# Value pages of five decode sequences: from the merge stage into the prompt's attention

## The reference

```python
k_past = pool_kv[l, page_table, :, 0].reshape(DB, past, FOX_H, HD)
v_past = pool_kv[l, page_table, :, 1].reshape(DB, past, FOX_H, HD)
r_past = swapaxes(cumsum(lf_past, axis=1, reverse=True) - lf_past, 1, 2)
s_p = einsum('bqhd,bshd->bhqs', q, k_past) * scale + a_new[..., None] + r_past[..., None, :]
s_n = einsum('bqhd,bshd->bhqs', q, kv[:, :, 0]) * scale + ...      # the new token's own key
p = masked_softmax(concatenate([s_p, s_n], -1))
o = einsum('bhqs,bshd->bqhd', p[..., :past], v_past) + einsum(..., p[..., past:], kv[:, :, 1])
```

## Time and profile before

| | us |
|---|---|
| median of 3 runs | 1461.28 |
| lowest and highest | 1459.33, 1465.89 |
| the profiled execution, whole | 1460.96 |
| its span | 1459.2 |
| PE busy in the span | 1209.6 (83%) |
| DVE busy | 801.3 (55%) |
| ACT busy | 240.1 (16%) |
| POOL busy | 173.7 (12%) |

### The profile page before, as it was taken

The page is one execution under the profiler, slowest core; times in us unless marked ns, Lnnn a source line. Parts: engine busy times, 40 slices in busy tenths (PEclk is TensorE's granted clock), DMA queues, the critical chain, the costliest instruction groups (busy, mean ns, idle before and its releaser), DMA issues. The chain is left out here.

```text
span 1459.2 us, 27607 instructions
## 1 busy us (share of the span) xinstructions
PE 1209.6 (83%) x10095; PEld 824.0 (56%) x10095; DVE 801.3 (55%) x1186; ACT 240.1 (16%) x681; POOL 173.7 (12%) x149
## 2 busy tenths in 40 slices
PE   0755677999999687998878998989796979798995
PEld 0755566886887474555556875546463645454241
DVE  1344340398999833456672457485857586725023
ACT  0000041112111201334451110100101010100113
POOL 0000000110000000000004031405050505040000
PEclk9968878999999765889999999989998999998898
DMA  8898504277888715100008449798978788676740
GB/s 224 243 305 245 198 31 145 88 240 231 282 268 300 198 23 203 44 1 1 1 1 262 136 143 324 232 304 259 318 233 278 239 296 275 229 235 212 265 190 30
DMA packets 205702, 282.01 MB, mean 193 GB/s; under 512 B 21614, under 2 KB 126599, under 8 KB 205119
## 3 DMA queue, kind: packets, MB, share of 16 engines
q1 hardware_dynamic: 109758, 202.40, 41.4%
q10 hardware_dynamic: 89376, 60.01, 14.3%
q0 software_dynamic: 6432, 17.83, 3.8%
HBM read 273.26 MB, written 11.11 MB: 195 GB/s over the span
## 5 line engine op out<-in xcount | busy, mean ns | idle before, releaser
L1581 PE MATMUL bank<-xnT,e_wg 128*128 128x260 f32 x1152 | 280.8, 402 | 0.5 <-DMA e_wg<-in_w_in 0.5
L1581 PEld LDWEIGHTS bank<-xnT,e_wg 128*128 128x128 f32 x1152 | 227.3, 200 | 76.5 <-issue 28.5
L585 PE MATMUL score_banks<-xnT,oT 128*128 128x260 f32 (+1 forms) x864 | 198.2, 388 | 9.9 <-DMA oT<-in_w_in 9.9
L1565 POOL DMA_INDIRECT d_slc<-in_cache_nsa_slc,selrow x128 | 154.5, 1207 | 380.2 <-PE score_banks L1652 336.1
L585 PEld LDWEIGHTS score_banks<-xnT,oT 128*128 128x128 f32 (+1 forms) x864 | 162.3, 190 | 40.3 <-DMA oT<-in_w_in 10.1
L249 PE MATMUL score_banks<-c_cols,c_w 64*64 64x64 f32 (+1 forms) x4096 | 96.5, 253 | 96.0 <-issue 57.0
L249 PEld LDWEIGHTS score_banks<-c_cols,c_w 64*64 64x64 f32 x4096 | 91.6, 166 | 100.7 <-issue 100.7
L1589 PE MATMUL bank<-oT,e_wb 128*128 128x512 f32 x192 | 101.1, 676 | 23.3 <-DVE cst L1843 11.8
L299 DVE COPY c_cols<-oT 128x1024 f32<-128x1024 f32 x48 | 48.9, 1146 | 101.2 <-DMA oT<-in_cache_nsa_cmp 82.0
L1614 PE MATMUL bank<-d_vpage,d_pf 128*8 128x512 f32 x512 | 80.0, 637 | 20.5 <-DMA d_vpage<-in_cache_fox_kv 20.5
L1589 PEld LDWEIGHTS bank<-oT,e_wb 128*128 128x128 f32 x192 | 40.0, 216 | 82.8 <-issue 82.6
(11 more groups left out here) (367 smaller groups left out, 1430.5 us busy)
## 6 DMA issues: line engine op xcount, KB each, us to landing
d_vpage<-in_cache_fox_kv SPq DMA_DIRECT2D x256, 256.0 KB, 4.7
d_kpage<-in_cache_fox_kv SPq DMA_DIRECT2D x96, 256.0 KB, 5.2
oT<-in_cache_fox_kv SPq DMA_DIRECT2D x80, 256.0 KB, 4.0
mt<-in_cache_fox_kv SPq DMA_DIRECT2D x80, 256.0 KB, 3.7
e_wg<-in_w_in ACTq DMA_DIRECT2D x36, 512.0 KB, 6.0
oT<-in_cache_nsa_cmp SPq DMA_DIRECT2D x128, 128.0 KB, 3.8
oT<-in_w_in ACTq DMA_DIRECT2D x13, 1024.0 KB, 7.9
oT<-in_cache_nsa_cmp ACTq DMA_DIRECT2D x64, 128.0 KB, 3.6
```

Of the source, the lines that this page charges most:

```text
L585: last = nc.tensor.matmul(pj[ch.n % 2][i][0:ch.w, 0:NM if ch.mem else TH], w[:, c, ch.off:ch.off + ch.w], rhs, start=c == 0, stop=c == DC - 1)
L1565: nc.gpsimd.indirect_dma_start(out=slc[:, n, :], out_offset=None, in_=k.cache_slc, in_offset=bass.IndirectOffsetOnAxis(ap=k.selrow[:, at:a ...
L1581: last = nc.tensor.matmul(gate_bank[n % 2][:, 0:TH], wg[product % WR][:, c, :], k.xnT[:, c, part * TH:(part + 1) * TH], start=c == 0, stop ...
```

## The change

The five early-scored sequences leave the last stage's fox work.

- In `middle`, their 5 x 32 pages of scores become probabilities at once: DVE adds the cumulated gates to `k.sfe`, takes the maximum per sequence and head, PE transposes and spreads it, DVE subtracts, ACT takes Exp, DVE sums, PE adds over partitions, DVE multiplies by the reciprocal. The last hidden product is cut in three pieces, with the new PE steps between them, and some copies and additions on DVE move up.
- In `prompt`, SP loads their 160 value pages into `mt` (four groups of two pages), and PE multiplies one quad of pages ahead of the transposes of each of the units 4 to 48, with a fold (adding the bands and turning) after each sequence's eight quads. The output transfers are issued between the page loads, one after every third quad. `mt` is no longer a buffer for transposed probabilities: two tiles `f_pt0`, `f_pt1` with three instead of four tiles of rows take its place, and the fourth tile of a unit is copied apart into a free corner of the tile. There is one output bank instead of two; the other holds the page sums.
- In `sample_and_merge`, key scores of the three late sequences run in steps 0 to 5, their fox softmax in steps 2, 4 and 6, their values in steps 3 and 4, 5 and 6, and 7. The other steps' softmax covers three kinds. The tail has no page values. `w_out` is loaded in two halves, the first when the last key page has been scored.

```diff
@@ middle, PE @@
-                hidden(3)
+                hidden(3, 0, 8)
+                te.wait_ge(x_max, 1)
+                te.wait_ge(grow_done, 2)
+                nc.tensor.transpose(fox_max, fmx[:, :, :].rearrange("p b h -> p (b h)"), k.ident).then_inc(x_turned, 1)
+                hidden(3, 8, 12)
+                te.wait_ge(x_dia, 1)
+                nc.tensor.matmul(fox_spread, k.ones[0:EH, :], fdia[:, :], start=True, stop=True).then_inc(x_spread, 1)
+                hidden(3, 12)
...
+                te.wait_ge(x_rden, 1)
@@ middle, ACT @@
+                sc.wait_ge(x_shifted, 1)
+                nc.scalar.activation(k.sfe[:, :, :, :], k.sfe[:, :, :, :], ACT.Exp).then_inc(x_exp, 1)
@@ middle, DVE @@
+                nc.vector.tensor_tensor(early, early, k.rpast[:, 0:EARLY * PAGES, :].rearrange("p (b n) h -> p b n h", b=EARLY), ALU.add).then_inc(x_scored, 1)
...
+                nc.vector.tensor_reduce(fmx[:, :, :], by_head, AX, ALU.max).then_inc(x_part, 1)
...
+                nc.vector.tensor_tensor(early, early, over_pages(fox_spread), ALU.subtract).then_inc(x_shifted, 1)
...
+                ve.wait_ge(x_exp, 2)
+                nc.vector.tensor_reduce(fden[:, :, :], by_head, AX, ALU.add).then_inc(x_part, 1)
...
+                nc.vector.tensor_tensor(early, early, frd[:, :, :].unsqueeze(2).to_broadcast([P, EARLY, PAGES, H]), ALU.mult).then_inc(x_done, 1)
@@ prompt, SP @@
-                for dst, src in outs:
+                left = list(outs)
+                for at in range(0, EARLY * PAGES, 2 * KV):
...
+                        if i % KV == 0 and n >= VG:
+                            sp.wait_ge(v_free, n - VG + 1)
+                        sp.dma_start(vpage[:, (n % VG) * KV + i % KV, :].unsqueeze(1),
+                                     k.cache_fox[bass.ds(pg, 1), :, 1, :].rearrange("a p n -> p a n")).then_inc(v_in[n % VG], 16)
+                    if at // (2 * KV) % 3 == 2 and left:
+                        sp.dma_start(*left.pop(0)).then_inc(out_done, 16)
@@ prompt, PE @@
-                    bank, done = o_bank[u.group % 2], ends_group(u)
-                    if u.group >= 2 and u.kind != "win":
-                        te.wait_ge(o_out[u.group % 2], u.group // 2)
+                    bank, done = o_bank, ends_group(u)
+                    if u.group and u.kind != "win":
+                        te.wait_ge(o_out[(u.group - 1) % 2], (u.group - 1) // 2 + 1)
...
+                    for i in range(4):
+                        n, page = (b * PAGES + 4 * g + i) // KV, 4 * g + i
+                        if i % KV == 0:
+                            te.wait_ge(v_in[n % VG], 16 * KV * (n // VG + 1))
+                        last = nc.tensor.matmul(fv_bank[32 * i:32 * i + H, :], k.sfe[:, b, page, :], vpage[:, (n % VG) * KV + i % KV, :],
+                                                start=g == 0, stop=g == QUAD - 1, skip_group_check=True)
...
+                    if u.no in work_of:
+                        b, g = work_of[u.no]
+                        if g < QUAD:
+                            page_values(b, g)
+                        else:
+                            fold(b)
                     turn(u)
@@ sample_and_merge @@
-        first_step = lambda b: 1 + (b - EARLY) * GROUPS // PER
+        first_step = lambda b: (b - EARLY) * GROUPS // PER
+        fox_of = {first_step(b) + 2: b for b in range(EARLY, NB)}
...
+            if b + 2 < NB:
+                values_at[b + 1] = (fox_no(b), 0, GROUPS // 2)
+                values_at[b + 2] = (fox_no(b), GROUPS // 2, GROUPS)
+            else:
+                values_at[b + 1] = (fox_no(b), 0, GROUPS)
...
                 small_values(LASTB)
+                turn_fox(sums_after[LASTB], LASTB - 1)
                 turn_sums(LASTB - 1)
-                page_values(LASTB, 0, 3)
                 y_products(0, 0)
-                page_values(LASTB, 3, 5)
                 y_products(0, 1)
-                page_values(LASTB, 5, 8)
                 y_products(1, 0)
```

More of the change, by code:

```diff
@@ L876, in _, with hidden @@
             def _(te):
-                def hidden(i):
+                def hidden(i, begin=0, end=STEP):
                     te.wait_ge(w1_in[i % 3], 64 * (i // 3 + 1))
                     te.wait_ge(tokens_done, 2)
-                    for d in range(STEP):
+                    for d in range(begin, end):
                         for v in range(2):
@@ L961, in _ @@
                                  start=True, stop=True).then_inc(v_done, 1)
+                te.wait_ge(x_den, 1)
+                nc.tensor.matmul(fox_den, k.ones, fden[:, :, :].rearrange("p b h -> p (b h)"), start=True, stop=True).then_inc(x_spread_den, 1)
                 te.wait_ge(kp_out, 2)
@@ L1205, in prompt, with turned_parts, probability @@
         both = lambda u: k.score_banks[:, 2 * (u.no % 2):2 * (u.no % 2) + 2, 0:u.n]
-        pt_bank, o_bank = ps[4:6], ps[6:8]
-        def transposed(u, j):
-            if u.kind == "mem":
-                return pt[u.set_no % 2][:, 0, 0:u.n // P, u.tile(j) * P:(u.tile(j) + 1) * P]
-            return pt[u.set_no % 2][:, j, 0:u.n // P, u.t * P:(u.t + 1) * P]
+        pt_bank, o_bank, fv_bank = ps[4:6], ps[6], ps[7]
+        of_turned = fv_bank[:, 0:8]
+        def turned_parts(u, j):
+            at = u.tile(j) * P
+            own = pt[u.set_no % 2][:, 0 if u.kind == "mem" else j]
+            tiles = min(u.n // P, 3)
+            parts = [(own[:, 0:tiles, at:at + P], in_bank(u, j)[:, 0:tiles])]
+            if u.n // P == 4:
+                parts.append((own[:, 1, 0:P], in_bank(u, j)[:, 3]))
+            return parts
+        def probability(u, j, t):
+            own = pt[u.set_no % 2][:, j]
+            return own[:, 1, 0:P] if t == 3 else own[:, t, t * P:T]
         def result(u):
@@ L1223, in _ @@
             def _(sp):
-                for dst, src in outs:
+                left = list(outs)
+                for at in range(0, EARLY * PAGES, 2 * KV):
+                    _, pages = nc.values_load_multi_w_load_instructions(k.table[0:1, at:at + 2 * KV], engines=[sp.engine], min_val=0, max_val=POOL - 1)
+                    for i, pg in enumerate(pages):
+                        n = (at + i) // KV
+                        if i % KV == 0 and n >= VG:
[4 more added lines that the diff above has]
+                        sp.dma_start(*left.pop(0)).then_inc(out_done, 16)
+                for dst, src in left:
                     sp.dma_start(dst, src).then_inc(out_done, 16)
@@ L1308, in place @@
                         ve.wait_ge(o_done, u.set_no - 1)
-                    nc.vector.tensor_copy(transposed(u, 0), in_bank(u, 0)).then_inc(pt_left, 1)
+                    for dst, src in turned_parts(u, 0):
+                        last = nc.vector.tensor_copy(dst, src)
+                    last.then_inc(pt_left, 1)
                 def result_out(u):
@@ L1342, in place @@
                         sc.wait_ge(o_done, u.set_no - 1)
-                    nc.scalar.activation(transposed(u, 1), in_bank(u, 1), ACT.Copy).then_inc(pt_right, 1)
+                    for dst, src in turned_parts(u, 1):
+                        last = nc.scalar.activation(dst, src, ACT.Copy)
+                    last.then_inc(pt_right, 1)
                 def result_out(u):
@@ L1656, in turn_sums @@
                 def turn_sums(b):
-                    te.wait_ge(of_out, b + 1)
                     te.wait_ge(os_out, b * 2 + 2)
-                    after(te, placed, b * 4)
-                    for c in range(4):
-                        nc.tensor.matmul(of_turned[:, 2 * c:2 * c + 2], fvs[:, c * P:(c + 1) * P], k.fold[:, 2 * c:2 * c + 2], start=True, stop=True)
+                    after(te, placed, b * 2)
                     for br in range(2):
@@ L1665, in turn_sums, with turn_fox @@
                     last.then_inc(sums_turned, 1)
+                def turn_fox(f, b):
+                    te.wait_ge(of_out, f + 1)
+                    te.wait_ge(placed, b * 2)
+                    after(te, fox_placed, f * 2)
+                    for c in range(4):
+                        last = nc.tensor.matmul(of_turned[:, 2 * c:2 * c + 2], fvs[:, c * P:(c + 1) * P], k.fold[:, 2 * c:2 * c + 2], start=True, stop=True)
+                    last.then_inc(fox_turned, 1)
                 def y_products(t, i, chunks=range(DC)):
-                    te.wait_ge(wout_in, 16)
+                    te.wait_ge(wout_in, 32)
                     te.wait_ge(mt_done, 2 * DC)
```

277 lines of the change are left out of this document (187 added, 90 removed).

## The result

The changed kernel takes 1477.1 us (median of 4 runs, 1473.68 to 1489.01), the kernel before 1462.24 beside it: a ratio of 1.0126 with a 95% interval of 1.0089 to 1.0162 (the medians alone give 1.0102). Slower by a little over 1%, where +10 us on 1461, 0.7%, was forecast. The profiled execution of the changed kernel took 1473.68, its span is 1471.9, 12.7 above that of the kernel before.

The account below looks back on a forecast made before the run. PE was taken to bound the prompt stage and the first part of last-stage steps, DVE their second part. Middle +4.5, prompt +49.5 and last stage -44 gave +10 on 1460.96: 1471 us, range 1442 to 1500.

Parts of the forecast that it names:

- Middle stage: Middle stage: added DVE passes mostly lie in waits, Exp and the sum behind it do not; +4.5 us, bounds 1 to 8.
- The term for the Exp: Middle stage: Exp on ScalarE, estimated at 1.4 to 2.9 us, has no cover and delays the block scores.
- Quads, folds, filled waits: Prompt stage: quads, first quads and folds add 53.1 us of PE work; filling PE's waits for ScalarE's copy returns 16.6.
- Clock: Prompt stage: filled pauses bring back some half-clock time, -7 us, bounds -13 to +13.
- The rival by the clock: Prompt stage: quads with few columns raise half-clock time from about 54 to over 100 us; 1491 or 1498; chance 0.13.
- Queue: Prompt stage: page loads wait behind outputs on SP's queue, +18 us, bounds 0 to 25; half-clock restart afterwards +2.
- Pages "just enough": Prompt stage: refilling a freed page buffer takes 7.9 us, within the 8.3 of two units, without slack.
- Last stage: Last stage: steps -25 us with the clock, tail -19; sum -44, bounds -58 to -30.
- Step 6: Last stage: without 18.3 us of key scores PE bounds all of this step, so it gains 8 us, not 18.
- Step 0: Last stage: takes 18.3 us of key scores on DVE, free because DVE waits 31.3 us there for the gates.
- The tail: End of last stage: the last sequence's page values leave the output products, -19 us, bounds -14 to -23.
- Step 7: Last stage: selected rows are asked for earlier, shortening DVE's 12.8 us wait; -5 us, between 0 and -10.

Follow-up runs that it names:

- run 4: Kernel before, value pages of the first five sequences neither loaded nor multiplied in the last stage: 1447.7 us, ratio 0.9897.
- run 5: Kernel before, the last sequence's value pages in the tail neither loaded nor multiplied: 1440.3 us, ratio 0.9898.
- run 8: Changed kernel with a ring of twelve pages, and the window state's copy and the fox rows issued in the middle stage: 1450.8 us, ratio 0.9955.
- run 6: Changed kernel with the window state's copy issued at the end of SP's list in the middle stage: 1467.0 us, ratio 1.0060.
- run 1: Changed kernel with the window state's copy issued by ScalarE on its own queue at unit 34: 1484.6 us, ratio 1.0126.
- run 11: Changed kernel with the window state's copy issued by GpSimd as one transfer of long pieces: 1485.0 us, ratio 1.0176.
- run 10: Changed kernel with the window state's copy issued by GpSimd as two transfers in pieces of 512 B: 1470.6 us, ratio 1.0081.
- run 2: Changed kernel with PE waiting for all four pages of a quad before its first product: 1483.4 us, ratio 1.0139.
- run 7: Changed kernel with a ring of twelve value pages in the prompt stage in place of eight: 1472.6 us, ratio 1.0120.
- run 12: As run 8, with SP issuing a value group ahead of the key groups in each last-stage step: 1451.2 us, ratio 0.9931.
- Run 3: Changed kernel with only the first eight value pages loaded in the prompt stage, all products kept, outputs issued at its start: 1440.6 us, ratio 0.9863.

## Why the prediction was right, and where it was off

The forecast was 1471 and its range held the time. The balance that decided it is shown: quads removed from the last stage's steps give back about a third of their PE time (run 4), the tail all of it (run 5), and in the prompt stage they are on the path (run 8: +30.9 us with no wait left). That the sum came within 3 us is luck, though: the terms below missed on both sides.

- **Middle stage**, +2.0 against +4.5. The term for the Exp was too large: it took 1.27 us, and DVE waited 0.7 there. The reductions took 2.45 us, not 1.43; a pass of the key scores was the wrong row for a reduction across the pages. The waits of the earlier trace rows covered the difference: of their 20.0 us only the last is left, with 4.6, and one of 3.7 has come.
- **Quads, folds, filled waits**: 53.1 less 16.6, nearly as worked out: with no wait for pages (run 8) PE is idle for 6.5 us of the stage, 21.2 before, so 14.7 of the 16.6 were filled. No wait of the transposes for ScalarE's copy was left.
- **Clock**, -7. By the granted clock of the stage (0.87 to 0.92) half-clock time fell from 55 to 44 us, of which some 12 are the long wait itself; that is some 10 us won. The rival by the clock did not come.
- **Queue**, +18 and +2: 15.1 in one wait, 19.4 in all, where and as long as worked out, just behind the state copy; the next longest, 2.7, follows the 2 MB of fox rows (issued at 648.77), where 3 was worked out. After the long wait PE ran at half clock for 5 us, which costs some 2.5 by half (an estimate). The reason was only half right. The copy makes the wait (run 6), but it need not stand ahead in the same queue (runs 1 and 11). The Trainium skill ("DMA: Bandwidth & Descriptors", on queues, rings and completion order) says that an engine goes round its queues packet by packet and finishes a packet before it turns to the next. If the packets that the trace counts are these, runs 1, 10 and 11 agree: in the copy of long pieces 64 packets have 65 KB and take 2.4 us each, with waits of 15.2 and 14.4 us; 2,080 packets of at most 4 KB gave no wait over 2.73, with the reservations of run 10. The same page of the Trainium skill (section "Issuing engines are not separate DMA queues") says that transfers of all issuing engines run on the same 16 engines; I weighed its rule on ring order and passed over that one.
- **Pages "just enough"**, 7.9 of 8.3 us: this is the step that failed, by some 14 us (13.9 in the split quads; in run 2 14.7 of waits besides the long one). The 8.3 was a mean over units. Of the four units of a set the first ones are short, two quads start 2.4 to 3.3 us apart there (711.72 and 714.76 in the trace after), so the ring of eight was empty again and again; and where the second pair is late, the quad's products take their time twice (by run 2 this costs about as much as the wait alone would). The ring of twelve ends these waits (run 7). The prediction had put this term at nothing.
- **Last stage**: steps -33.4 against -25. Step 6 gave 13.3, not 8. Without key scores PE is busy 51.8 of its 55.2 us, so it is PE-bound as foreseen, but PE's own work there had shrunk to less than I had taken from the earlier trace rows. Of the 33.4 the quads alone are 11 by the profile of run 4; what the key scores and the smaller softmax gave was not run by itself. Step 0 was 2.7 longer, not free: DVE waited 7.0 us there for key pages that are now needed at once. The tail gave 20.9 against 19. Step 7 gave 1.4, not 5: DVE still waits 12.0 us for the selected rows, 12.8 before. Its row, from DVE's waits in step 7 after:

```profile
DVE d_kpage L2039 <- DMA d_slc<-in_cache_nsa_slc,selrow: 12.0, 1, 12.0
```

So 10 us were forecast and 12.7 measured in the profiled execution, 15 by the medians, with the prompt stage 12 us over its term and the others together 10 under theirs.

## What to carry to other kernels

Before work is moved from one stage to another, ask of each stage which engine ends it, and price the work by that stage: here 49 us of PE time were worth some 15 in the steps, where DVE ends the part that holds most of them. In the tail the quads were worth all their time. Where PE ends the stage, 53 us of PE work cost 31, since it filled waits and the clock was higher. A ring is sized by its shortest gaps, not by the mean. A big copy between DRAM tensors belongs where no load is waited for; here another queue did not take it out of the way.

## What was not expected of the hardware

Kernels that differ little ran the prompt stage at granted clocks from 0.88 (runs 7 and 11) to 0.95 (run 12), some 25 to 68 us at half clock, which by half of the difference is worth some 20 us (an estimate). Run 3, in which PE hardly waits, got 0.89. I have no rule for it from these runs; it stays open, and single stage lengths are to be read with the clock beside them.

Issuing 4 MB in pieces of 512 B held ScalarE for 16.9 us, where one transfer of long pieces took 0.84.
